# Small experts multiply their weights unsplit, two feature blocks side by side

## The reference

```python
def swiglu(h, w_gate, w_up, w_down):
    return (jax.nn.silu(h @ w_gate) * (h @ w_up)) @ w_down

def moe_swiglu(h, w_router, w_gate, w_up, w_down):
    logits = (h @ w_router).astype(jnp.float32)
    top_vals, top_idx = lax.top_k(logits, TOP_K)          # TOP_K = 2 of 8
    top_w = jax.nn.softmax(top_vals, axis=-1)
    combine = jnp.sum(jax.nn.one_hot(top_idx, N_EXPERTS, dtype=jnp.float32) * top_w[..., None], axis=-2)
    y = jnp.zeros_like(h)
    for e in range(N_EXPERTS):
        y = y + combine[..., e:e + 1] * swiglu(h, w_gate[e], w_up[e], w_down[e])
    return y
```

## Time and profile before

| | us |
|---|---|
| median of 3 runs (1440.64 to 1440.73) | 1440.68 |
| the profiled execution's own time | 1441.36 |
| its span, first to last instruction | 1439.6 |
| PE busy | 1421.6 (99%) |
| weight loads of PE busy | 1154.7 (80%) |
| DVE busy | 1169.4 (81%) |
| ACT busy | 989.4 (69%) |
| POOL busy | 55.4 (4%) |

### The profile page before, as it was taken

One profiled execution on the slowest core, in us unless ns is written; L12 is line 12 of the kernel. 1 busy time (PEld: TensorE's weight loads), 2 busy tenths in 40 slices (PEclk: granted clock), 3 DMA queues, 4 the chain that ended last, 5 costly groups with the idle time before them and its releaser, 6 DMA issues.

```text
span 1439.6 us, 17466 instructions
## 1 busy us (share of the span) xinstructions
PE 1421.6 (99%) x6728; PEld 1154.7 (80%) x6728; DVE 1169.4 (81%) x1050; ACT 989.4 (69%) x991; POOL 55.4 (4%) x61
## 2 busy tenths in 40 slices
PE   9999999999999999999999999999999999999997
PEld 8977888888887788887778887778887778888885
DVE  5777755556677769889999889999889999899896
ACT  6566553434565668778887778887778877777774
POOL 1000000000000009200000000000000000002000
PEclk9999999999999999999999999999999999999999
DMA  9933655546653369999999999999999999999991
GB/s 350 376 102 120 203 179 201 183 140 197 200 173 125 127 236 370 422 396 371 422 421 421 422 420 393 421 422 420 422 421 395 418 422 421 421 397 375 421 382 56
DMA packets 96489, 460.08 MB, mean 320 GB/s; under 512 B 7656, under 2 KB 13304, under 8 KB 53392
## 3 DMA queue, kind: packets, MB, share of 16 engines
q1 hardware_dynamic: 91632, 444.63, 78.8%
q10 hardware_dynamic: 3312, 9.46, 1.8%
q0 software_dynamic: 1456, 4.79, 0.9%
HBM read 447.85 MB, written 11.01 MB: 319 GB/s over the span
## 4 chain that ended last, share of the span: by engine, by line
PE 83%; DVE 8%; ACT 4%; issue 3%; DMA 2%; SPq 0%; ACTq 0%; DVEq 0%
PE A L498 15%; PE A L500 15%; PE A L499 15%; PE DN L498 5%; PE DN L500 5%; PE DN L499 5%; DVE wlo L472 4%; PE A L504 3%; PE A L505 3%; PE DN L2016 2%; ACT whi L465 2%; DVE wlo_more L472 1%; DMA raw_more<-in_moe_w_down 1%; PE T L2030 1%; PE DN L504 1%
## 5 line engine op out<-in xcount | busy, mean ns | idle before, releaser
L472 DVE TENSOR_TENSOR wlo<-raw,whi 128x2048 fp32r<-128x2048 f32 (+1 forms) x252 | 563.8, 2251 | 124.2 <-ACT whi L465 123.6
L465 ACT ACTIVATE whi<-raw 128x2048 fp32r<-128x2048 f32 (+1 forms) x252 | 472.0, 1885 | 158.9 <-PE A L500 83.3
L472 DVE TENSOR_TENSOR wlo<-raw_more,whi 128x2048 fp32r<-128x2048 f32 x74 | 168.2, 2288 | 11.1 <-ACT whi L465 10.8
L498 PE MATMUL A<-whi,hTh 128*128 128x512 f32 (+2 forms) x448 | 174.4, 389 | 0.8 <-DVE wlo L472 0.7
L499 PE MATMUL A<-wlo,hTh 128*128 128x512 f32 (+2 forms) x448 | 169.9, 379 | 0.0
L500 PE MATMUL A<-whi,hTl 128*128 128x512 f32 (+2 forms) x448 | 169.8, 379 | 0.0
L498 PE MATMUL A<-whi,heTh 128*128 128x512 f32 x420 | 166.5, 396 | 0.0
L500 PE MATMUL A<-whi,heTl 128*128 128x512 f32 x420 | 163.9, 390 | 0.0
L499 PE MATMUL A<-wlo,heTh 128*128 128x512 f32 x420 | 163.6, 390 | 0.0
L465 ACT ACTIVATE whi<-raw_more 128x2048 fp32r<-128x2048 f32 x74 | 140.6, 1916 | 23.1 <-PE A L500 9.6
L472 DVE TENSOR_TENSOR wlo_more<-raw,whi_more 128x2048 fp32r<-128x2048 f32 x57 | 130.4, 2287 | 19.2 <-ACT whi_more L465 19.2
(11 more groups left out here) (367 smaller groups left out, 2314.4 us busy)
## 6 DMA issues: line engine op xcount, KB each, us to landing
raw<-in_moe_w_up SPq DMA_DIRECT2D x79, 1024.0 KB, 11.3
raw<-in_moe_w_down SPq DMA_DIRECT2D x78, 1024.0 KB, 12.7
raw<-in_moe_w_gate SPq DMA_DIRECT2D x77, 1024.0 KB, 12.9
raw_more<-in_moe_w_gate SPq DMA_DIRECT2D x35, 1024.0 KB, 13.5
raw_more<-in_moe_w_down SPq DMA_DIRECT2D x34, 1024.0 KB, 13.5
raw_more<-in_moe_w_up SPq DMA_DIRECT2D x33, 1024.0 KB, 12.5
raw<-in_w_in SPq DMA_DIRECT2D x22, 1024.0 KB, 6.8
raw<-in_dense_w_down SPq DMA_DIRECT2D x11, 1024.0 KB, 4.9
```

The costliest lines, as they stand in the source:

```text
L465: nc.scalar.activation(split_slot(u, e)[0][:, :n], raw_of(u, e)[:, :n], ACT.Copy).then_inc(hi_done, 1)
L472: nc.vector.tensor_tensor(lo[:, :n], raw_of(u, e)[:, :n], hi[:, :n].bitcast(F32), ALU.subtract).then_inc(lo_done, 1)
L498: nc.tensor.matmul(o, hi, wh, start=start, stop=False)
```

## The change

In turns 1, 3 and 5 all 42 units are now used whole, where it was four. The tokens of a small expert are held once, in full precision, in 64 columns (`heTf`, `aTf`); there are no low parts of tokens, of activations or of weights. `side_by_side` issues two full-precision matmuls: an even block of 128 input features goes to rows 0 to 63 of the result, the odd block next to it to rows 64 to 127. The sum over both halves is made as before by `fold`, by turning, and at the end by L1528 and L1530. Of the tokens of a small expert 64 rows are loaded instead of 128. Counts of semaphores for the low parts of tokens and activations now count large experts alone (`large_before`); in small ones TensorE waits for ScalarE's copy in their place. Lines of the changed kernel are shifted by some (L504 and L505 became L505 and L506, L585 became L590).

```diff
-WHOLE = [e * EU + down_at(j, EG) + 1 for e in SMALL_AT for j in (0, 2, 4, 5)]
+WHOLE = [e * EU + i for e in SMALL_AT for i in range(EU)]
...
-        aTp, aTr = aTh[:, :, :, :SMALL], aTh[:, :, :, SMALL:]
+        aTf = place("aTf", [P, 2, 4, SMALL], F32, o_o + 8192)
...
+        heTf = place("heTf", [P, KD, SMALL], F32, o_g)
...
-        def stacked(o, hi_lo, wh, wl, start, stop):
-
-            nc.tensor.matmul(o, hi_lo, wh, start=start, stop=False)
-            return nc.tensor.matmul(o, hi_lo, wl, start=False, stop=stop)
+        def side_by_side(o, even, odd, w_even, w_odd, start, stop):
+
+            nc.tensor.matmul(o[:SMALL], even, w_even, start=start, stop=stop)
+            return nc.tensor.matmul(o[SMALL:], odd, w_odd, start=start, stop=stop)
...
-                        act.dma_start(he[:], by_slot[(e + 1) * P:(e + 2) * P, :]).then_inc(he_landed, 16)
+                        w = SMALL if is_small(n, e + 1) else P
+                        act.dma_start(he[:w, :], by_slot[(e + 1) * P:(e + 1) * P + w, :]).then_inc(he_landed, 16)
...
-                            ahead.to(u + 6)
                             act.wait_ge(folded, folds(e, j))
...
-                    if j:
+                    if j and not few:
                         dve.wait_ge(ff_hi[1], EG * n + j + e * EG)
...
-                        tokens_low(j - EG + 1, n + 1, e, T[0], is_small(n, e + 1))
+                        if not is_small(n, e + 1):
+                            tokens_low(j - EG + 1, n + 1, e, T[0])
...
+                def whole_products(u, h, bank, border=False):
+
+                    pe.wait_ge(raw_landed[raw_at(u, e)], raw_there(u, e))
+                    w = raw_of(u, e)
+                    for kk in range(0, 4, 2):
+                        k = 4 * h + kk
+                        if border:
+                            pe.wait_ge(he_hi, 8 * e + k + 2)
+                        last = side_by_side(bank, heTf[:, k, :], heTf[:, k + 1, :], w[:, kk * N:(kk + 1) * N],
+                                            w[:, (kk + 1) * N:(kk + 2) * N], k == 0, k == KD - 2)
                     last.then_inc(unit_used, 1)
...
-                def whole_down(u, i, q):
+                def whole_down(u, j, i, q):
 
                     pe.wait_ge(raw_landed[raw_at(u, e)], raw_there(u, e))
-                    for kk in range(2):
-                        k = 2 * i + kk
-                        for h in range(2):
-                            c = kk * D + h * N
-                            last = nc.tensor.matmul(DN[h][:], aTh[:, q, k, :].bitcast(F32), raw_of(u, e)[:, c:c + N],
-                                                    start=False, stop=u == base + EU - 1 and kk == 1)
+                    w = raw_of(u, e)
+                    for h in range(2):
+                        last = side_by_side(DN[h], aTf[:, q, 2 * i, :], aTf[:, q, 2 * i + 1, :],
+                                            w[:, h * N:(h + 1) * N], w[:, D + h * N:D + (h + 1) * N],
+                                            j == 1 and i == 0, j == EG and i == 1)
                     last.then_inc(unit_used, 1)
```

More of the change, by code:

```diff
@@ L528, in is_small, with large_before @@
             return n == 0 and e in SMALL_AT
+        def large_before(n, e):
+            return e - sum(s < e for s in SMALL_AT) if n == 0 else n - len(SMALL_AT) + e
         def folds(e, j):
@@ L915, in _, with tokens_high @@
             first.to(UM + S)
-            def tokens_high(i, n, e, bank, w=P):
+            def tokens_high(i, n, e, bank, few=False):
                 act.wait_ge(gathered, 2 * n + i + 1 + e * 2)
+                w = SMALL if few else P
                 for kk in range(4):
@@ L1989, in expert @@
                 few = is_small(n, e)
+                large = large_before(n, e)
                 def products(u, h, bank, border=False):
@@ L1995, in products @@
                         if border:
-                            pe.wait_ge(he_lo, 8 * n + k + 1 + e * 8)
+                            pe.wait_ge(he_lo, 8 * large + k + 1)
                         wh, wl = split_tile(u, kk, N, e=e)
[L1998 to L2001, removed]
+                        last = product(bank[:], heTh[:, k, :], heTl[:, k, :], wh, wl, k == 0, k == KD - 1)
+                    last.then_inc(unit_used, 1)
+                def whole_products(u, h, bank, border=False):
[7 more added lines that the diff above has]
+                                            w[:, (kk + 1) * N:(kk + 2) * N], k == 0, k == KD - 2)
                     last.then_inc(unit_used, 1)
@@ L2025, in turn_gated @@
                         pe.wait_ge(cw_out, spreads(n, e))
-                    if j > 2:
-                        pe.wait_ge(ff_lo[1], EG * n + j - (2 if j < EG else 1) + e * EG)
+                    if j > 2 and few:
+                        pe.wait_ge(ff_hi[1], EG * e + j - (2 if j < EG else 1))
+                    elif j > 2:
+                        pe.wait_ge(ff_lo[1], EG * large + j - (2 if j < EG else 1))
                     for k in range(4):
@@ L2042, in expert @@
                         for h in range(2):
-                            products(u + h, h, A[j % 2], j == 0)
+                            (whole_products if few else products)(u + h, h, A[j % 2], j == 0)
                     if j:
@@ L2053, in expert @@
                     if following and j == EG:
-                        pe.wait_ge(he_lo, 8 * n + 12 + e * 8)
+                        if is_small(n, e + 1):
+                            pe.wait_ge(he_hi, 8 * (e + 1) + 4)
+                        else:
+                            pe.wait_ge(he_lo, 8 * large_before(n, e + 1) + 4)
                         turn_tokens(1, e + 1)
@@ L2063, in expert @@
                     if following and j == EG - 1:
-                        pe.wait_ge(ff_lo[1], EG * n + EG - 2 + e * EG)
+                        if few:
+                            pe.wait_ge(ff_hi[1], EG * e + EG - 2)
+                        else:
+                            pe.wait_ge(ff_lo[1], EG * large + EG - 2)
                         turn_tokens(0, e + 1)
@@ L2069, in expert @@
                             pe.wait_ge(oe_dve, e)
-                        pe.wait_ge(ff_lo[1], EG * n + j + e * EG)
+                        if few:
+                            pe.wait_ge(ff_hi[1], EG * e + j)
+                        else:
+                            pe.wait_ge(ff_lo[1], EG * large + j)
                         ud = base + down_at(j - 1, EG)
                         for i in range(2):
[L2073 to L2082, removed]
+                            if few:
+                                whole_down(ud + i, j, i, q)
+                            else:
+                                pe.wait_ge(lo_done, split_before(ud + i, e) + 1)
+                                for kk in range(2):
+                                    k = 2 * i + kk
+                                    for h in range(2):
+                                        wh, wl = split_tile(ud + i, kk, D, h * N, N, e)
+                                        last = product(DN[h][:], aTh[:, q, k, :], aTl[:, q, k, :], wh, wl,
                                                        j == 1 and k == 0, j == EG and k == 3)
[L2084 to L2087, removed]
+                                last.then_inc(unit_used, 1)
                             if j == EG - 1 and i == 0:
```

28 lines of the change are left out of this document (11 added, 17 removed).

## The result

The changed kernel takes 1443.36 us (median of 15 runs, 1441.89 to 1445.78), the kernel before 1440.78 us beside it (15 runs). The ratio is 1.0018, with an interval of 1.0011 to 1.0025: slower, by more than can be put down to the measurement. 1440.5 us and no change were forecast; the time is within the range given, the sign of the difference is not the forecast's.

What follows compares the result with a forecast made beforehand. TensorE and DMA were both taken as full, with large turns starting when data allow. TensorE's 6.2 us gain per small turn is given back waiting for loads: -0.2 us in sum, 1440.5 us predicted, eight-in-ten range 1432 to 1446.

Steps and rivals of the forecast that it cites:

- Rival 3: Small turns: halves not fully side by side; 1638 us if nothing overlaps, 1491 if weight loads stand bare; chance 0.11.
- A small turn of 92.2 us on TensorE: Small turns: 72.2 us units, 15.8 turning and folding, 4.2 switching between halves and full array; 6.2 us less than before.
- Fewer matmuls: Small turns: a sign of the forecast being right; no size given.
- Unit 51 issued at 658.6, landed at 664.1: Turn 1: the load waits for TensorE's use of unit 42, is issued 5.3 us later than before, lands 5.5 later.
- Then 33 units at 2.49 and two half-megabyte tiles, 84.7: unit 84 lands at 748.8: Loads from unit 51's landing to that of unit 84, first of turn 2: 84.7 us; before, landed at 747.4.
- The pair: One small and one large turn together, paced by loads, lag and buffer waits: 217.05 us, before 217.65.
- Turn 6 starts when its data allow, not when the small turn leaves TensorE free: Head of turn 6, kernel before: TensorE starts 6.7 us behind unit 252's landing, held by splits and token copies.
- 6.3 us of lag: Heads of large turns: time from the first unit's landing to TensorE's start, 0.42 us less than before.
- untouched: Turns 6 and 7 (118.8 and 119.2 us) and the last 12.2 us stay as before.
- Rival 1: Small turns: TensorE's gain arrives whole, 18.6 us, giving 1422.1 us; chance 0.06.
- Rival 2: Weight loads: buffer waits are hidden and DMA alone sets the pace; 8.5 us saved, 1432.2 us; chance 0.19.
- Rival 4: Loads after a buffer wait: restart takes 6.9 us, costing 1.4 us three times, 1444.7 us; chance 0.09.

Runs made afterwards that it cites:

- the lending kernel: The changed kernel, with the tenth to thirteenth unit of each small turn loaded into the idle `whi` and `wlo` as four more buffers: 1434.44 us, ratio 0.9953.

## Why the prediction was right and wrong

The mechanism was forecast: the gain appears on TensorE and is given back at the loads. What failed is the size of its terms, for the answer is a small difference of large ones.

- A pair of matmuls in 0.43 us, a unit in 1.72: right (0.43 in the timeline; 1.77 and 1.72 for units 42 and 43). Rival 3 was wrong in both its forms: both blocks in one half gave 1635 us, so the changed kernel's halves do overlap, and a small turn of 90.5 us leaves no room for bare weight loads (115.2).
- A small turn of 92.2 us on TensorE: 90.5 from its first product to the next turn's (656.62 to 747.10, the changed kernel with half its bytes), so the gain is 7.8 and not 6.2. The 4.2 us for going between halves and full array were too many: (90.5 - 72.2 - 15.8) / 28 = 0.09 us each, not 0.15. It had no effect on the time, since the loads hide it.
- "Fewer matmuls" as a sign of being right: there are none fewer, 6728 records in both pages. A unit has 8 records either way; only their overlap is new.
- Unit 51 issued at 658.6, landed at 664.1: 658.74 and 663.8. The restarts at units 135 and 219 land after 5.1 us too, not 5.5.
- **"Then 33 units at 2.49 and two half-megabyte tiles, 84.7: unit 84 lands at 748.8"**: this step failed, by its size. It took 86.1 us, and unit 84 landed at 749.9; behind units 135 and 219 the same term took 85.4 and 84.8. The stream was not slow there. The DMA engines moved 36.05 MB from landing 51 to landing 84, where the term has 35.65 (33 units, 34.6, and two tiles):

```profile
DMA packets 5017, 36.05 MB, mean 419 GB/s; under 512 B 556, under 2 KB 556, under 8 KB 684
...
q1 hardware_dynamic: 4868, 35.46, 99.3%
q10 hardware_dynamic: 144, 0.52, 1.5%
```

  One of the tiles was through before; but the weights' queue, q1, moved 0.9 MB more than 33 units hold. These bytes can only belong to units behind 84, which were on their way when it landed. The term counted landings as if each load had the DMA engines to itself. That this is why unit 52 came 5.3 us behind unit 51 is likely, but no run tests it. A price of the empty queue alone it is not. In the lending kernel the stream never stops (DMA share 1.01), and its unit 84 lands 86.0 us behind its unit 51 all the same, with this moved in between:

```profile
DMA packets 5093, 36.04 MB, mean 419 GB/s; under 512 B 570, under 2 KB 570, under 8 KB 826
```

- The pair: 217.05 forecast, 217.6 and 216.9 measured. Unit 252: 1182.9 forecast, 1184.4 measured.
- "Turn 6 starts when its data allow, not when the small turn leaves TensorE free": wrong for the kernel before, as its own timeline and its run with half its bytes show. Of the lag of 6.7 us read from the earlier trace rows the data need 4.3, and the rest is TensorE still at work on turn 5. In the changed kernel the forecast's 6.3 us of lag and 118.6 of turn 2 came as 4.3 and 120.7. The sums, 124.9 and 125.0, agree, and that is luck: two errors cancel. TensorE's idle time at a head was 4.4 us, not 6.2.
- From landing 252 to the end: 0.4 less than before was forecast, for the shorter lag; measured are 257.1 against 256.9, 0.2 more. The prediction called turn 6 "untouched" and so left TensorE's clock at full, though it had TensorE idle for 6.2 us in its own sum; it did not ask what the clock does then. With the clock kept full by dummy products the same way takes 256.7 us, so the half clock makes about 0.5 of these 0.6 us.
- The sum, against the profiled executions: unit 252 + 1.7 (forecast + 0.2), behind it + 0.2 (forecast - 0.4), together + 1.9 to the span where - 0.2 stood. The profiled execution of before was 0.6 above its median and that of the changed kernel on it, which makes 2.6 of the medians.
- Rival 1 (the whole gain, 1422.1) was wrong, but it is what TensorE has to give: 1418.0 with the loads out of the way. Rival 2 (the stream never stands, 1432.2) is what the lending kernel comes near to, 1434.4, so the pace of DMA alone was about right. Rival 4 (a dearer restart, 1444.7) is nearest in time but not in cause: it had the first load behind a wait land after 6.9 us, and it landed after 5.1.

Open: how much of the 2.6 us is half clock. The traces with and without it differ by 0.2 to 0.5 us, the medians by 1.3, with an interval as wide.

## What to carry to other kernels

Where TensorE and the DMA engines are both full, an edit that saves work on one of them is worth what the other leaves; halve the bytes once, with all partitions kept, and the other's share is known. Before calling late data the bound, look whether TensorE stands idle at that place at all. When an edit moves the release of a buffer from an early reader to a late one, run that part alone: here it cost 6.2 us. Take the time from one landing to a far one from rows, not from megabytes over the full rate: here the two are 1.4 us apart, half of the whole difference. Buffers that the edit leaves idle are the place to win the loss back.

## What the runs showed of the hardware

- The two column halves of the array ran at once in both orders of issue that were tried: sixteen records of 512 columns in 3.65 us, 6.9 when all write one half. The weight loads, 137 ns each in the earlier trace rows, were hidden in either case: the records stay 0.43 us apart, in twos or singly.
- A load of 1 MB and one of half its partitions took the same time (210 to 222 GB/s at a DMA share of 0.97 and 0.98). Half the bytes on all partitions lowered the share to 0.75 in the kernel before.
- At the end of each of the three waits of 4.4 us TensorE's granted clock fell to half: 0.5 us before the next product at turn 2, 0.5 behind it at turn 4, 1.5 before it at turn 6. It stayed there for 3.4, 3.4 and 6.8 us. With products of no use in the wait it stayed at full.
- With the DMA engines busy all the time between (share 0.98, 363 GB/s), unit 52 landed 5.3 us behind unit 51; further on in the same stream the step is 2.5.
